# A hybrid attention, SSD and expert layer: final norm in pieces between the ninth unit's dots, last unit in groups of two and one, residual by TensorE, first loads in smaller steps

## The chip, the core and the metric

The kernel runs on one core of one Trainium2 chip. The metric is the device time of one execution in microseconds (us); the time of a kernel is the median of its runs. All data are 32-bit floats.

## The reference, cut to what matters

256 tokens of width 1024 go through one layer:

```python
mix = token_mix(x, positions, w_in, ...)      # top-k attention + SSD scan, then @ w_out
x = layer_norm(ALPHA * x + mix, ln1_g, ln1_b)
ffn = peer(x, peer_wq, k1, k2, u, v)          # 8 heads, 16 of 16384 experts each, per token
x = layer_norm(ALPHA * x + ffn, ln2_g, ln2_b)

# peer, per token: for each of 8 x 16 chosen experts e with gate g_e
ffn = sum_e gelu(dot(x, u[e])) * g_e * v[e]
```

Each token needs 128 rows of `u` and of `v`. The kernel keeps them side by side in HBM as one table `expert_uv`, a row of 2048 floats (8 KB) for each expert.

## The kernel before, in words

The tokens are two tiles of 128 (one token per partition). The projections, the attention and the SSD scan of tile 0 come first, and those of tile 1 are woven into the first expert units.

**Units and slots.** The expert part is 16 units (`UNITS`): unit u is head u % 8 of tile u // 8, with 16 slots. A slot is one gather (L459): an indirect DMA that POOL issues and that puts one 8 KB row into each of 128 partitions, into one of 16 places of `arena`. POOL waits before it until the place is free (`slot_used`, L457). DVE takes the dot of the row's first half with the token (L1548, `dot_slots`), ACT the gelu (L994) and the product with the gate (L999), each for a group of slots (`slot_groups`, L337: four groups of four, in the last unit 4, 4, 2, 2, 1, 1, 1, 1). ACT then scales the row's second half in place (L1009), and PE adds it into two PSUM banks of the tile by eight transposes against the identity (L659, `sum_slots`), which frees the place. In the program of DVE each unit begins with the routing of the next one (`route_sides`, `route_pairs`), some 10 us of short instructions, and then takes its dots.

**Units 9 to 14** run in a hardware loop on each engine (`LOOP_FIRST`, `LOOP_TURNS`), the others are written out.

**End of a tile.** The banks hold the sum transposed. ACT copies them out (`copy_sum`, L1016), PE transposes them back into banks 6 and 7 (`sum_back`, L669), DVE adds the scaled residual (`add_sum`, L1539) and takes statistics (`half_stats`, L1377), centres with the gain (`centre`, L1386), waits for ACT's root (`root_of_variance`, L947) and spreads (`spread`, L1394); SP stores. For tile 0 PE does this after all slots of unit 8 (L810 to L813) and DVE after the dots of unit 8 (L1607 to L1610). The gain and offset of this norm are loaded by SP, spread over 128 partitions by the DMA (L404, L405).

**The last unit** has no transposes. ACT makes a diagonal matrix of each slot's weights (L1006), and PE adds diagonal x row straight into banks 6 and 7 (`sum_last_slots`, L679), after `sum_back(1)` has opened them. Each of the 32 products runs as two passes, as do all products of 32-bit data here but the transposes, so the profile counts 64.

**The front.** SP loads the columns of x in four parts and the q weights in two halves (L371, L373) while ACT loads the index weights in four parts and nine small tensors; PE projects the index columns of tile 0, then of tile 1 (L692), waiting for a part at every second k (L487), and then q (L695). SP's further weight loads wait for all small tensors (L374 to L376).

## Time and profile before

| | |
|---|---|
| three runs, median (lowest to highest) | 805.42 us (805.28 to 806.05) |
| profiled execution, its own time | 807.17 us |
| its span | 805.4 us |
| busy: PE, DVE, ACT, POOL | 549.3, 548.6, 450.2, 283.9 us |
| moved by DMA | 301.08 MB, 374 GB/s over the span |
| mean granted TensorE clock | 0.843 of full speed |

Times in the profile are us from the span's start. PE's busy time are its matmul passes, PEld its weight loads. The DMA share is the mean busy share of 16 DMA engines. An idle time stands with what ended it; idle time of an engine that sets nothing costs nothing.

### The profile page before, as it was taken

What the parts mean: (1) busy time and instruction counts of PE and PEld (TensorE: products, weight loads), DVE (VectorE), ACT (ScalarE), POOL (GpSimd) and SP (SyncE); (2) the same over time, 40 slices, a digit from 0 to 9 for tenths busy, and PEclk for the clock granted to TensorE, in tenths of its full rate; (3) what the DMA queues carried; (4) which work ended last, traced back from release to release, by engine and by line L of the source; (5) the groups of instructions that cost most, each with busy time, mean ns of one, the idle gap of its engine ahead of it and who ended that gap; (6) DMA issues with size and microseconds to landing.
All of it is one profiled execution on the core that took longest, in us unless ns stands there. A gap on an engine that the chain in (4) does not pass through costs nothing.

```text
span 805.4 us, 10125 instructions
## 1 busy us (share of the span) xinstructions
PE 549.3 (68%) x3340; PEld 455.4 (57%) x3340; DVE 548.6 (68%) x1395; ACT 450.2 (56%) x805; POOL 283.9 (35%) x267
## 2 busy tenths in 40 slices
PE   7999999998957878565545454609554645454695
PEld 4486497776857778454445454608454644454642
DVE  3488487898654767676757576399767767676554
ACT  1125138778744666666565566529665656566532
POOL 0000004536613345444434444307644444444400
PEclk9999999999978989867878787758777668777689
DMA  7992017999999999999999999999999999999992
GB/s 258 390 392 90 0 54 239 422 421 421 422 418 421 420 421 420 421 421 422 419 422 420 422 421 422 421 422 360 421 421 422 423 422 421 422 423 422 422 422 111
DMA packets 51433, 301.08 MB, mean 374 GB/s; under 512 B 5696, under 2 KB 8000, under 8 KB 17600
## 3 DMA queue, kind: packets, MB, share of 16 engines
q0 software_dynamic: 36864, 268.45, 80.6%
q1 hardware_dynamic: 12144, 30.67, 10.2%
q10 hardware_dynamic: 2384, 1.44, 0.6%
q8 instruction: 22, 0.36, 0.2%
q14 instruction: 19, 0.16, 0.0%
HBM read 299.49 MB, written 1.05 MB: 373 GB/s over the span
## 4 chain that ended last, share of the span: by engine, by line
DMA 45%; DVE 20%; PE 19%; issue 8%; ACT 5%; POOL 3%; DVEq 0%; SPq 0%; another core or an unknown queue 0%; POOLq 0%; ACTq 0%
DMA arena<-in_expert_uv,expert 43%; PE bank L488 5%; DVE arena L1548 4%; PE bank L679 4%; PE bank L659 3%; POOL arena L459 3%; ACT arena L1009 2%; PE bank L500 2%; PE bank L603 2%; DMA ln_gb<-in_w_in 2%; ACT weight L999 1%; PE bank L622 1%; DVE score L1527 1%; DVE picked L1528 1%; DVE big L1258 1%
## 5 line engine op out<-in xcount | busy, mean ns | idle before, releaser
L659 PE MATMUL bank<-ident,arena 128*128 128x128 f32 x1920 | 299.2, 325 | 237.1 <-ACT arena L1009 235.7
L459 POOL DMA_INDIRECT arena<-in_expert_uv,expert x256 | 282.2, 1102 | 479.2 <-PE bank L659 261.9
L1548 DVE SCALAR_TENSOR_TENSOR arena<-x_sb,arena 128x1024 f32<-128x1024 f32 x256 | 307.0, 1224 | 172.6 <-DMA arena<-in_expert_uv,expert 165.1
L659 PEld LDWEIGHTS bank<-ident,arena 128*128 128x128 f32 x1920 | 275.1, 171 | 263.1 <-ACT arena L1009 258.6
L1009 ACT ACTIVATE arena<-arena,weight 128x1024 f32<-128x1024 f32 x240 | 257.5, 1141 | 2.2
L994 ACT ACTIVATE gelu<-dots 128x4 f32<-128x4 f32 (+2 forms) x76 | 15.6, 205 | 223.6 <-DVE arena L1548 214.4
L999 ACT ACTIVATE weight<-gelu,gate 128x1 f32<-128x1 f32 x256 | 56.1, 286 | 3.5
L488 PE MATMUL bank<-arena,x_t 128*128 128x512 f32 (+1 forms) x128 | 53.8, 576 | 4.8 <-DMA x_t<-in_x_columns 4.8
L488 PEld LDWEIGHTS bank<-arena,x_t 128*128 128x128 f32 x128 | 25.3, 203 | 27.0 <-issue 25.3
L622 PE MATMUL bank<-x_t,arena 128*128 128x128 f32 x256 | 29.9, 275 | 0.0
L679 PE MATMUL bank<-arena,mid 128*128 128x512 f32 x64 | 29.4, 622 | 0.0
L622 PEld LDWEIGHTS bank<-x_t,arena 128*128 128x128 f32 x256 | 29.2, 192 | 0.0
L500 PE MATMUL bank<-x_t,arena 128*128 128x128 f32 x256 | 29.0, 275 | 0.0
L500 PEld LDWEIGHTS bank<-x_t,arena 128*128 128x128 f32 x256 | 28.7, 192 | 0.1
L603 PE MATMUL bank<-arena,big 128*128 128x512 f32 x64 | 28.5, 592 | 0.0
L994 ACT ACT_TABLE_LOAD x19 | 24.4, 1283 | 0.6
L679 PEld LDWEIGHTS bank<-arena,mid 128*128 128x128 f32 x64 | 12.8, 202 | 15.9 <-issue 15.2
L1548 DVE DVE_READ_ACCUMULATOR arena<-x_sb,arena 128x1 f32 x256 | 21.2, 83 | 0.0
L357 ACT ACT_TABLE_LOAD x15 | 19.2, 1283 | 0.7
L603 PEld LDWEIGHTS bank<-arena,big 128*128 128x128 f32 x64 | 11.8, 190 | 12.9 <-issue 12.9
L622 PE MATMUL bank<-x_t,mix 128*128 128x128 f32 x128 | 15.1, 276 | 0.0
L622 PE MATMUL bank<-x_t,big 128*128 128x128 f32 x128 | 14.9, 275 | 0.0
(227 smaller groups left out, 488.9 us busy)
## 6 DMA issues: line engine op xcount, KB each, us to landing
arena<-in_w_in SPq DMA_DIRECT2D x5, 2048.0 KB, 17.5
arena<-in_w_out SPq DMA_DIRECT2D x2, 2048.0 KB, 19.3
arena<-in_expert_uv,expert POOLq DMA_INDIRECT x256, 28.1
arena<-in_peer_wq SPq DMA_DIRECT2D x4, 1024.0 KB, 9.4
mix<-in_peer_wq SPq DMA_DIRECT2D x2, 1024.0 KB, 5.2
big<-in_peer_wq SPq DMA_DIRECT2D x2, 1024.0 KB, 4.9
arena<-in_w_idx ACTq DMA_DIRECT2D x4, 304.0 KB, 5.7
x_t<-in_x_columns SPq DMA_DIRECT2D x4, 256.0 KB, 5.2
```

The lines of the kernel that those rows point to most:

```text
L357: nc.scalar.activation(gate_e[:, :], best[:, :], ACT.Exp, bias=neg_best[:, :], accum_out=gate_sum[:, :]).then_inc(gate_exp_ready, 1)
L459: pool.indirect_dma_start(out=arena[:, slot * SLOT:(slot + 1) * SLOT], out_offset=None, in_=expert_uv, in_offset=bass.IndirectOffsetOnAxis ...
L488: last = mm(bank(job)[:, 0:width], lhsT=x_t[:, k, t * P:(t + 1) * P], rhs=weight_rows(name, k, width), start=k == 0, stop=k == KT - 1)
L500: last = mm(bank(job)[:, c * P:(c + 1) * P], lhsT=weight_rows(f"xbc{n}", k)[:, c * P:(c + 1) * P], rhs=x_t[:, k, t * P:(t + 1) * P], start ...
L603: last = mm(bank(job)[:, :], lhsT=mix_t[t][:, k, :], rhs=weight_rows(f"out{half}", k), start=k == 0, stop=k == KT - 1)
L622: last = mm(bank(job)[:, n * P:(n + 1) * P], lhsT=head_weights(h)[:, k, n * P:(n + 1) * P], rhs=h_t[:, k, t * P:(t + 1) * P], start=k == 0 ...
L659: last = mm(banks[2 * tile + k // 4][:, (k % 4) * P:(k % 4 + 1) * P], lhsT=arena[:, at + k * P:at + (k + 1) * P], rhs=ident[:, :], is_tran ...
L679: last = mm(banks[SUM_BACK + half][:, :], lhsT=diag[:, j % 8, :], rhs=arena[:, at:at + 512], start=False, stop=j == SLOTS - 1, skip_group_ ...
L994: run(gelu[:, parity, part], dots[:, parity, part], ACT.Gelu).then_inc(gelu_ready, 1)
L999: done = run(weight[:, parity, j:j + 1], gelu[:, parity, j:j + 1], ACT.Copy, scale=gate[:, parity, j:j + 1])
L1009: run(arena[:, at:at + D_MODEL], arena[:, at:at + D_MODEL], ACT.Copy, scale=weight[:, parity, j:j + 1]).then_inc(scaled_ready, 1)
L1548: ins = stt(rows, x_rows[:, bass.ds(tile * D_MODEL, D_MODEL)], 1.0, rows, ALU.mult, ALU.mult, accum_out=dots[:, parity, j:j + 1])
```

## The change

It moves the final norm of tile 0 into unit 8's dots, changes the order and the group sizes of the last unit, gathers the last two slots' halves apart, lets PE add the residual as a product with ALPHA x identity, loads the final norm's vectors as four short rows that PE spreads over the partitions in unit 5, and loads the first operands in five parts, with q's weights laid out in HBM so that a partition's part is one piece of 8 KB.

```diff
@@ slot_groups, loads (SP; ACT's w_idx loads likewise)
                 elif u == UNITS - 1:
-                    sizes = (4, 4, 2, 2, 1, 1, 1, 1)
+                    sizes = (2,) * 4 + (1,) * 8
+        IDX_PARTS = [range(0, 1), range(1, 2), range(2, 4), range(4, 6), range(6, 8)]
-            for part in range(4):
-                ks = slice(2 * part, 2 * part + 2)
+            for part, some in enumerate(IDX_PARTS):
+                ks = slice(some[0], some[-1] + 1)
                 sp.dma_start(x_t[:, ks, :], ...).then_inc(idx_in[part], 16)
             for half in range(2):
-                sp.dma_start(q_halves[half], w_rows[:, 4 * half:4 * half + 4, Q0:Q0 + 512]).then_inc(w_in_sem["q"], 16)
+                sp.dma_start(q_halves[half], w_q[half].rearrange("p (k n) -> p k n", k=4)).then_inc(w_in_sem["q"], 16)
...
-            sp.wait_ge(ln1_done, 1)
-            sp.dma_start(ln_gb[:, 0, :], cast_rows(ln2_g)).then_inc(ln2_in, 16)
-            sp.dma_start(ln_gb[:, 1, :], cast_rows(ln2_b)).then_inc(ln2_in, 16)
+            sp.wait_ge(y_ready, TILES)
+            for n, source in enumerate((ln2_g, ln2_b)):
+                sp.dma_start(ln2_rows[2 * n:2 * n + 2, :], source.rearrange("(a b) -> a b", a=2)).then_inc(ln2_in, 16)
@@ POOL
-            gather_unit(UNITS - 1, 1)
+            gather_unit(UNITS - 1, 1, SLOTS - 2)
+            u, half_rows = UNITS - 1, expert_uv.rearrange("e (s d) -> (e s) d", s=2)
+            pool.wait_ge(last_rows_ready, 1)
+            for part in range(2):
+                for n in range(2):
+                    j = SLOTS - 2 + n
+                    at = slots_of(u)[j] * SLOT + part * D_MODEL
+                    if part == 0:
+                        pool.wait_ge(slot_used, (u - 1) * SLOTS + j + 1)
+                        pool.sem_inc(rows_asked, 1)
+                    pool.indirect_dma_start(
+                        out=arena[:, at:at + D_MODEL], out_offset=None, in_=half_rows,
+                        in_offset=bass.IndirectOffsetOnAxis(ap=last_rows[:, n, part:part + 1], axis=0),
+                    ).then_inc(last_values_in[n] if part else rows_in[slots_of(u)[j]], 16)
@@ PE
+            def add_residual(t):
+                pe.wait_ge(alpha_ready, 1)
+                for half in range(2):
+                    mm(banks[SUM_BACK + half][:, :], lhsT=alpha_ident[:, :], rhs=x_sb[:, t, half * 512:(half + 1) * 512],
+                       start=True, stop=False, skip_group_check=True)
...
+            def spread_ln2(part):
+                job = ("ln2", part)
+                pe.wait_ge(ln2_in, 2 * 16)
+                wait_bank(pe, job)
+                mm(bank(job)[:, :], lhsT=ident[0:4, part:part + 1].broadcast_to([4, P]), rhs=ln2_rows[0:4, :],
+                   start=True, stop=True).then_inc(full(job), 1)
...
-            for t in range(TILES):
-                project(("proj_idx", t), "idx", t, IDX_COLS + SSD_HEADS)
+            for part, some in enumerate(IDX_PARTS):
+                pe.wait_ge(idx_in[part], 32)
+                for t in range(TILES):
+                    project(("proj_idx", t), "idx", t, IDX_COLS + SSD_HEADS, ks=some)
...
-            sum_slots(PEER_HEADS, 1, first_unit=True)
+            sum_group(PEER_HEADS, 0)
             for n in range(4, PSUM_BANKS):
                 pe.wait_ge(bank_free[n], bank_uses[n])
+            add_residual(0)
             sum_back(0)
+            for g in range(1, 4):
+                sum_group(PEER_HEADS, g)
...
             pe.wait_ge(sum_added, 2)
+            add_residual(1)
+            sum_last_slots(UNITS - 1, range(0, 4))
             sum_back(1)
-            sum_last_slots(UNITS - 1)
+            sum_last_slots(UNITS - 1, range(4, SLOTS))
@@ ACT (copy_sum(1) stands after group 1 of the last unit, the root of tile 0 after group 2 of unit 8)
+            act.wait_ge(decay_masked, TILES)
+            run(alpha_ident[:, :], ident[:, :], ACT.Copy, scale=ALPHA).then_inc(alpha_ready, 1)
+            def take_ln2(part):
+                job = ("ln2", part)
+                wait_job(act, job)
+                act.wait_ge(ln1_done, 1)
+                run(ln_rows[:, part * 512:(part + 1) * 512], bank(job)[:, :], ACT.Copy).then_inc(free(job), 1)
...
@@ DVE (add_sum is gone; centre reads the banks for the final norm)
+            def sum_stats(t, half):
+                dve.wait_ge(half_back[half], 1 + 2 * t)
+                link(nc.vector.bn_stats(stats[:, 6 * half:6 * half + 6], banks[SUM_BACK + half][:, :]))
...
+                crossing = isinstance(u, int) and u == PEER_HEADS
                 for g in range(len(slot_groups(u))):
                     dot_slots(u, tile, parity, g)
                     if g == 0 and not last:
                         finish_gate(u + 1, 1 - parity)
+                    if crossing and g == 1:
+                        sum_stats(0, 0)
+                    if crossing and g == 2:
+                        sum_stats(0, 1)
+                        dve.wait_ge(ln2_ready, 4)
+                        centre(0, summed=True)
+                if crossing:
+                    spread(0, TILES, result_ready)
...
+            for part in range(2):
+                ins = ts(last_rows[:, :, part], expert[:, 1, SLOTS - 2:], 2.0, float(part), ALU.mult, ALU.add)
+            ins.then_inc(last_rows_ready, 1)
             dot_unit(UNITS - 1, TILES - 1, 1)
             for half in range(2):
-                half_stats(TILES - 1, half, add_sum)
-            normalise(TILES - 1, 2 * TILES - 1, result_ready)
+                sum_stats(TILES - 1, half)
+            normalise(TILES - 1, 2 * TILES - 1, result_ready, summed=True)
```

PE's `spread_ln2(g)` stands before group g of unit 5, ACT's `take_ln2(g)` behind it. In `sum_last_slots` slots 14 and 15 wait besides for `last_values_in`.

## Rows read from the trace of the kernel before

**Rows 1.** The page: the chain that ended last, by engine; the gathers' issue.
```profile
DMA 45%; DVE 20%; PE 19%; issue 8%; ACT 5%; POOL 3%; DVEq 0%; SPq 0%; another core or an unknown queue 0%; POOLq 0%; ACTq 0%
...
arena<-in_expert_uv,expert POOLq DMA_INDIRECT x256, 28.1
```

**Rows 2.** Windows: length; busy PE, PEld, DVE, ACT, POOL; clock; DMA share, GB/s.
```profile
300.00:400.00 100.00, 62.98 (x427) 59.16 (x425) 68.60 (x179) 64.53 (x109) 47.66 (x44) 0.81 1.01 421
545.00:550.00 5.00, 5.00 (x28) 5.00 (x27) 5.00 (x11) 4.93 (x10) 3.23 (x2) 0.54 0.75 264
550.00:555.00 5.00, 4.46 (x42) 4.22 (x41) 5.00 (x9) 4.93 (x9) 4.39 (x3) 1.00 1.00 370
555.00:560.00 5.00, 3.92 (x32) 3.13 (x31) 4.24 (x24) 4.93 (x10) 3.78 (x4) 1.00 0.97 383
```

**Rows 3.** Timeline at the crossing: start, length (us), engine, line, operation [idle before <-releaser].
```profile
490.82 1.06 ACT L1016 ACTIVATE mix<-bank 128x512 f32<-128x512 f32 x2
...
519.83 1.04 PE L669 MATMUL bank<-ident,mix 128*128 128x128 f32 x8
...
520.54 0.69 DVE L1539 SCALAR_TENSOR_TENSOR x_sb<-x_sb,bank 128x512 f32<-128x512 f32 x1 [9.03 <-issue]
...
536.58 1.23 DVE L1548 SCALAR_TENSOR_TENSOR arena<-x_sb,arena 128x1024 f32<-128x1024 f32 x1
...
546.47 1.66 POOL L459 DMA_INDIRECT arena<-in_expert_uv,expert  x1 [24.35 <-PE bank L659]
```

**Rows 4.** DMA issues: loads of ln_gb; the window behind the second pair.
```profile
ln_gb<-in_ln_g SPq DMA_DIRECT2D x2, 512.0 KB, 11.6
...
230.00:235.00 5.00, 0.00 (x0) 0.00 (x0) 1.23 (x2) 0.00 (x0) 0.00 (x0) 0.71 1.02 424
```

**Rows 5.** Timeline of the last unit and the tail.
```profile
755.53 6.46 PE L659 MATMUL bank<-ident,arena 128*128 128x128 f32 x32 [3.63 <-ACT arena L1009]
...
764.32 1.28 ACT L1006 ACTIVATE mid<-ident,weight 128x128 f32<-128x128 f32 x4
...
766.23 1.94 PE L669 MATMUL bank<-ident,mix 128*128 128x128 f32 x8 [4.25 <-ACT mix L1016]
...
767.96 29.36 PE L679 MATMUL bank<-arena,mid 128*128 128x512 f32 x64
...
791.65 1.23 DVE L1548 SCALAR_TENSOR_TENSOR arena<-x_sb,arena 128x1024 f32<-128x1024 f32 x1 [1.21 <-DMA arena<-in_expert_uv,expert]
...
793.48 0.40 ACT L1006 ACTIVATE mid<-ident,weight 128x128 f32<-128x128 f32 x1
...
796.50 0.69 DVE L1539 SCALAR_TENSOR_TENSOR x_sb<-x_sb,bank 128x512 f32<-128x512 f32 x1 [3.62 <-PE bank L679]
...
799.62 0.21 DVE L1383 BATCH_NORM_AGGREGATE moments<-stats 128x2 f32<-128x12 f32 x1
```

**Rows 6.** Windows of one us around PE's last transposes and its first weighted passes.
```profile
760.00:761.00 1.00, 1.00 (x7) 1.00 (x6) 0.61 (x2) 0.00 (x0) 0.99 (x1) 0.50 1.00 418
761.00:762.00 1.00, 0.98 (x8) 0.74 (x6) 0.14 (x1) 0.00 (x0) 0.70 (x2) 0.91 1.01 418
768.00:769.00 1.00, 1.00 (x3) 0.48 (x3) 0.06 (x2) 0.00 (x0) 0.00 (x0) 0.50 1.04 434
```

**Rows 7.** Timeline of the front.
```profile
4.81 11.12 PE L488 MATMUL bank<-arena,x_t 128*128 128x304 f32 x32 [4.81 <-DMA x_t<-in_x_columns]
...
12.67 0.17 DVE L1160 CAST pos_f<-pos_i 128x2 f32<-128x2 int32 x1 [12.67 <-DMA arena<-in_inv_freq]
...
16.32 3.70 PE L488 MATMUL bank<-x_sb,x_t 128*128 128x512 f32 x8 [0.39 <-DMA ln_gb<-in_w_in]
...
16.87 15.11 SPq L364 DMA_DIRECT2D arena<-in_w_in  x5
...
30.36 0.69 DVE L1185 TENSOR_TENSOR arena<-bank,sin_cos 128x512 f32<-128x512 f32 x1 [3.50 <-PE bank L488]
```

**Rows 8.** Window in which the q weights land.
```profile
12.00:14.00 2.00, 2.00 (x10) 1.47 (x9) 1.22 (x8) 0.00 (x0) 0.00 (x0) 1.00 0.95 315
```

More of the change, by code:

```diff
@@ L71, in psum_jobs @@
         jobs += [("peer_q", 0, h), ("key_scores", 0, h), ("peer_q", 1, h), ("key_scores", 1, h)]
-    return jobs
+    return jobs + [("ln2", part) for part in range(4)]
 def bank_plan():
@@ L218, in build_layer @@
         expert = ctx.enter_context(nc.sbuf_tensor("expert", [P, 2, 16], i32))
+        last_rows = ctx.enter_context(nc.sbuf_tensor("last_rows", [P, 2, 2], i32))
+        alpha_ident = upper
         gate_e, gate_sum = sb("gate_e", 16), sb("gate_sum", 1)
@@ L230, in build_layer @@
         x_in = sem("x_in")
-        idx_in = [sem(f"x_t_and_idx_in{part}") for part in range(4)]
+        IDX_PARTS = [range(0, 1), range(1, 2), range(2, 4), range(4, 6), range(6, 8)]
+        idx_in = [sem(f"x_t_and_idx_in{part}") for part in range(len(IDX_PARTS))]
         w_names = ["q", "k", "xbc0", "xbc1", "v", "z", "out1", "out0"] + [f"wq{h}" for h in range(PEER_HEADS)]
@@ L258, in build_layer @@
         SUM_BACK = 6
+        last_rows_ready, alpha_ready = sem("last_rows_ready"), sem("alpha_ready")
+        last_values_in = [sem(f"last_values_in{n}") for n in range(2)]
         result_ready, out_stored = sem("result_ready"), sem("out_stored")
@@ L439, in gather_unit @@
                     pool.wait_ge(experts_ready, u + 1)
-                for j, slot in enumerate(slots_of(u)):
+                for j, slot in enumerate(slots_of(u)[:n]):
                     if isinstance(u, int) and u == 0 and j == 8:
@@ L669, in sum_back, with sum_last_slots @@
                         last = mm(banks[SUM_BACK + half][:, n * P:(n + 1) * P], lhsT=sum_t[:, 4 * half + n, :], rhs=ident[:, :],
-                                  is_transpose=True, start=n == 0, stop=t == 0, skip_group_check=True)
+                                  is_transpose=True, start=False, stop=t == 0, skip_group_check=True)
                     last.then_inc(half_back[half], 1)
-            def sum_last_slots(u):
-                for j in range(SLOTS):
+            def add_residual(t):
[3 more added lines that the diff above has]
+                       start=True, stop=False, skip_group_check=True)
+            def sum_last_slots(u, some):
+                for j in some:
                     pe.wait_ge(diag_ready, j + 1)
+                    if j >= SLOTS - 2:
+                        pe.wait_ge(last_values_in[j - SLOTS + 2], 16)
                     for half in range(2):
@@ L803, in _ @@
                         queries(*now)
+                    if u == LN2_UNIT:
+                        spread_ln2(g)
                     sum_group(u, g)
@@ L817, in _ @@
             pe.wait_ge(sum_added, 2)
+            add_residual(1)
+            sum_last_slots(UNITS - 1, range(0, 4))
             sum_back(1)
-            sum_last_slots(UNITS - 1)
+            sum_last_slots(UNITS - 1, range(4, SLOTS))
         @block.scalar
         def _(act):
-            for part in range(4):
-                ks = slice(2 * part, 2 * part + 2)
+            for part, some in enumerate(IDX_PARTS):
+                ks = slice(some[0], some[-1] + 1)
                 act.dma_start(chunk(places["idx"], IDX_COLS + SSD_HEADS)[:, ks, :],
@@ L1024, in weigh_unit @@
                     weigh_slots(u, parity, g)
-                    if last and g == 0:
+                    if last and g == 1:
                         copy_sum(TILES - 1)
@@ L1028, in weigh_unit @@
                         copy_sum(0)
+                    if isinstance(u, int) and u == PEER_HEADS and g == 2:
+                        root_of_variance(TILES)
             take_index_dots(0)
@@ L1431, in _ @@
             for half in range(2):
-                half_stats(0, half, add_mixed)
+                half_stats(0, half)
             normalise(0, 0, h_ready)
@@ L1534, in finish_gate @@
                 ts(gate[:, parity, :], gate_e[:, :], gate_sum[:, :], None, ALU.mult).then_inc(gate_ready, 1)
-            def add_sum(t, half, part):
-                dve.wait_ge(half_back[half], 1 + 2 * t)
-                link(stt(x_sb[:, t, part], x_sb[:, t, part], ALPHA, banks[SUM_BACK + half][:, :], ALU.mult, ALU.add))
-                dve.sem_inc(sum_added, 1)
             def dot_slots(u, tile, parity, g):
@@ L1592, in _ @@
             for half in range(2):
-                half_stats(1, half, add_mixed)
+                half_stats(1, half)
             centre(1)
@@ L1605, in _ @@
                 dot_unit(u, u // PEER_HEADS, u % 2)
-                per_unit = count[0] - before + 1
-            dve.wait_ge(ln2_in, 32)
-            for half in range(2):
-                half_stats(0, half, add_sum)
-            normalise(0, TILES, result_ready)
+                if u < PEER_HEADS:
+                    per_unit = count[0] - before + 1
             dve.wait_ge(scores_ready, len(score_order))
```

36 lines of the change are left out of this document (22 added, 14 removed).

## The prediction

> **What bounds the kernel now.** I read the page's chain first [rows 1]: its largest share is DMA, which is the gathers of expert rows, and a gather lands 28.1 us after its issue, so some eleven are queued at once. The windows show whether that queue runs dry [rows 2]: over 300 to 400 us the DMA share is 1.01 at 421 GB/s while PE is busy 63 and DVE 69 of 100 us. A gather moves 128 rows of 8 KB, 1.05 MB, so one lands every 1.05 / 0.421 = 2.49 us. From there to the end the time is bytes over 421 GB/s. An edit pays there only if it removes bytes or refills a dry queue. What lies ahead of the first gather (compute) and behind the last one (the tail) counts in full.
>
> The same view shows one dry place: in 545 to 560 us the rate is 264, 370 and 383 GB/s [rows 2]. The timeline says why [rows 3]. DVE has no dot left after unit 8 and waits 9.03 us for the sum that PE hands back only after all of unit 8; it normalises, routes unit 10, and takes its next dot at 536.58. Slots are freed only after dots, so POOL's next issue waits 24.35 us.
>
> In the tail [rows 5] the last row lands at 791.65, its diagonal is ready at 793.88, but PE's string of 64 weighted passes runs from 767.96 without a gap to 797.32: there PE is the bound. It starts late because it stands behind the copy of the sum (ACT), which stands behind the first group of four.
>
> In front [rows 7], PE starts at 4.81 when the first index parts land, ends them at 15.93, and waits for the q weights until 16.32.
>
> A measurement of this kernel can tell about 0.2% (1.6 us) from no change.
>
> **The change, part by part.** Signs: minus is time saved.
>
> Middle norm. Missing bytes in the three windows: (421-264)x5 + (421-370)x5 + (421-383)x5 = 1230 KB, at 421 GB/s 2.9 us. After the change DVE's work is two BN_STATS, one aggregate, one add, two centring and two spreading passes, some 5 us, laid between unit 8's dots. A dot takes 1.23 us of each 2.49 us [rows 5], so 1.25 us per slot is free. The new wait is DVE's for the first half of the sum, behind group 1. ACT's copy starts at 490.82 [rows 3], PE then has its last scaled slot, four residual passes (0.43 us each, 0.85 at half clock; working below) and the turned-back transposes (1.04 us): ready at about 495.5 to 498, and DVE is there at about 491.7. Behind the wait stand dots 8 to 15, which are due from 492.9 on; they start 3 to 6 us late, and the eight of them regain up to 10 us. Nothing is late by group 3, except that unit 9's routing starts about 1.7 us later (the spreading). The cover is the queue: in the old kernel DVE was without dots for 25 us and this cost 2.9 us, so delays below some 22 us cost nothing. The root's two table loads on ACT are hidden in the same way. Ends: 0 (the stall comes back elsewhere) and -2.9; I take **-2.9**.
>
> Final norm's vectors. Before, two loads of 512 KB [rows 4] go through the full queue: in the five us behind their issue the rate is 424 GB/s at a share of 1.02 [rows 4]. Now four short rows come in and PE spreads them in unit 5. 2 x 524 KB / 421 GB/s = **-2.5 us**. Added: four 512-column products on PE and four copies on ACT of about 0.6 us, covered by PE's and ACT's idle time and the queue; without cover about 6 us. Ends: -2.5 and 0.
>
> Last unit. The time of one weighted pass: at the full clock 0.43 us, since 64 take 29.36 us with the first few at half clock (the window at 768 shows 0.50 [rows 6]); 64 x 0.43 = 27.5, so the slow start cost 1.9 us. A slot is 4 passes, 1.72 us. After the change PE goes on at 761.99, when its transposes of unit 14 end [rows 5], with four residual passes, slots 0 to 3 (diagonals at about 760 and 764), the turned-back sum, and the rest. Continuous work would end at 762.0 + 68 x 0.43 + 1.04 = 792.3, so it catches up with the data. Two things could then end last. Slot 13: a diagonal is ready 2.28 us behind its landing (791.65 to about 793.9), two gathers earlier than slot 15's: 788.95. From there slots 13, 14 and 15 take 3 x 1.72 and end at 794.1. The value halves: the last lands at 791.65 as before (same bytes), the one before it 1.25 us earlier, 790.4 + 3.44 = 793.8. The later counts; its first half bank is complete 0.86 us earlier, at 793.25. Before, DVE began at 796.50. **-3.2 us**. POOL's two further issues (about 0.94 us each, at 762 to 767) lie 25 us ahead of their landings. Its new wait for the row numbers is answered before unit 15's dots, so nothing queues behind it. Ends: -3.5, and -1.3 if PE pays the 1.9 us of slow clock again.
>
> The clock. In the old trace PE's transposes start at 755.53; the granted clock is 0.50 at 760 and 0.91 at 761 while only transposes run [rows 6]. The new residual passes follow at once, at the full level of 2.4 GHz. The Trainium skill (TensorE: Matmul & The Clock Gate, Part 4: PE-mode transpose) says that transposes do not count as busy for the gate. By that rule the residual would start at 1.2 GHz and the tail gain be 1.3 us instead of 3.2; the rows at 760 and 761 speak against it.
>
> The split gathers. Their price is not in this trace: no gather has 4 KB rows. Lower end nothing (the same bytes), upper end that a half takes as long as a whole one, 2 x 2.49 = +5.0 us. I take 0, since the nearest row, the window of q's loads with their 2 KB rows [rows 8], still shows three quarters of the rate with many small loads beside them, and the norm vectors' loads, with rows of 4 KB, left the rate at 424 GB/s [rows 4]. The Trainium skill (DMA: Bandwidth & Descriptors, Rules for kernel authors) asks for at least 1 MiB per DMA, and (section Anatomy of one DMA) gives some 2.0 us of fixed cost for each on the GpSimd path; paid in series by four halves that would be an estimated +8 us. Gathers here land 2.49 us apart although each needs 28.1 us, so such a cost overlaps.
>
> Residual by PE. Before: scale-add, statistics, scale-add, statistics from 796.50, aggregate at 799.62: 3.12 us. Now statistics read the bank: 0.69 us on half 0 while PE ends half 1 (0.86 us later), then 0.69 and small gaps: 1.6 us. **-1.5 us**; the centring reads PSUM, as the old scale-add did at 0.69 us. Ends -1.6 and -1.2.
>
> First loads. The first parts are half as large, so PE may start about 0.7 us earlier (a first pair of parts is 560 KB, at 315 to 421 GB/s 1.3 to 1.8 us, and half of it falls away) and end the index products near 15.2 by its 11.1 us of passes. Contiguous q weights: 2.1 MB at 315 GB/s [rows 8] is 6.7 us, at 421 it would be 5.0, so q lands near 14.6 to 15.5. PE starts q at about 15.4. SP and ACT each issue one load more, some 0.5 us, ahead of everything behind them; the queues are busy then, and SP's next issue waits for small loads until 16.87 anyway. Ends: +0.5 (a late last part) and -1.3; I take **-0.9**. It passes to the first gather, since the way there is compute.
>
> Sum: 2.9 + 2.5 + 3.2 + 1.5 + 0.9 = 11.0 us. The profiled execution took 807.17 us (span 805.4): 796.2. The three runs' median is 1.75 us lower, so 794.4.
>
> **Rivals.**
> 1. PE still bounds the tail (a half-clock spell or waits between small groups). For: 68 passes against 2.49 us per slot leave little; the clock stood at 0.50 at 768, after 4.25 us without work [rows 5, 6]. Against: PE has a backlog from 762 on. 2 to 3 us of the tail gain go: 796.4 to 797.4.
> 2. The stall at the crossing stays, because DVE waits for PE inside unit 8. For: a new chain ACT, PE, DVE. Against: 22 us of cover. 797.3.
> 3. Half gathers cost as much as whole ones: +5.0, 799.4. For: rows cost something each. Against: above.
> 4. Slower than before: the large q packets hold back ACT's small loads (positions, frequencies, keys), which share the engines. Place: DVE's first instruction at 12.67, SP's wait that ends at 16.87 [rows 7]. DVE has 3.50 us of idleness at 30.36, so the small loads must land over 3.5 us later to cost anything, and over 3.5 + 10.1 + 1.6 = 15.2 us later (behind about 28 us) to make the kernel slower. At most the 2.1 MB of q stand ahead of them, 5.0 us at 421 GB/s. Time with 17 us of delay: 794.4 + 0.9 + 17 - 3.5 = 808.8.
> 5. The change does not remove the bytes' cost (the load ran in spare bandwidth). Against: share 1.01. 796.9.
>
> **How the numbers follow.** Forecast 0.70, its own range 792.5 to 796; rival 1 0.13, rival 2 0.06, rival 3 0.05, rival 5 0.02, rival 4 0.02, and 0.02 that small losses together leave no difference. The range reaches from 792.0 (front at its best, tail at -3.5, and half a us for the sum) to 798.5, over rivals 1, 2 and 5, short of rival 3. Faster by over 0.2%: 0.96; within: 0.02; slower: 0.02.
>
> **What would show it.** Right: no window under 410 GB/s between 300 us and the last gathers; POOL's longest wait near 8 us in place of 24.35; 1 MB fewer bytes moved; from the last landing to the first store's issue some 4.7 us less than before; PE's q products start near 15.4; at the end PE shows short waits on DMA or on diagonals. Wrong: a gap of POOL over 15 us near unit 9, a granted clock of 0.5 within 20 us of the end, gathers in the last 5 us at under 350 GB/s, or an index part landing after 13.5 us.

## The result and the profile after

| | before | after |
|---|---|---|
| four runs each on one chip, median (lowest to highest) | 805.73 us (805.28 to 806.45) | 799.60 us (799.24 to 800.43) |
| profiled execution, its own time (span) | 807.17 us (805.4) | 799.47 us (797.7) |
| moved by DMA | 301.08 MB | 300.04 MB |
| mean granted TensorE clock | 0.843 | 0.853 |

The ratio on record is 0.9917 (95% interval 0.9904 to 0.9930); the two medians shown stand as 0.9924, 6.1 us apart. The forecast was 794.4 us in a range of 792.0 to 798.5: the sign was right, the time 1.1 us above the range. Between the two profiled executions the gain is 7.7 us; the profile of before lies 1.4 us above the median of its runs, that of after 0.1 us under its own.

**Where the 7.7 us lie.** The rows of DVE's dots are good milestones, since each dot waits for its row. From the timelines of both kernels I collected the starts of some:

```
start of DVE's dot (us)      before   after    shift
first dot of all             129.92   129.66   -0.26
unit 1, slot 15              216.61   216.20   -0.41
unit 3, slot 15              308.69   305.79   -2.90
unit 7, slot 15              470.57   467.07   -3.50
unit 8, slot 15              510.28   506.82   -3.46
unit 10, slot 15             592.91   589.41   -3.50
unit 15, slot 12             784.23   780.78   -3.45
DVE begins last statistics   796.50   790.14   -6.36
DVE aggregates them          799.62   791.81   -7.81
```

So the front gives 0.4 us, the stretch with the norm's vectors (from unit 1's slot 15 to unit 3's) 2.5, units 4 to 7 0.6, the last unit 2.9 and the statistics 1.5. The crossing (units 8 to 10), which I had counted on, gives nothing.

**The page after**: the chain by engine; POOL's gathers with their busy time and what ended POOL's idle time; the gathers' issues (KB and time to landing are not given where they vary).

```profile
DMA 54%; PE 17%; DVE 16%; issue 6%; ACT 4%; POOL 2%; SPq 0%; DVEq 0%; POOLq 0%; ACTq 0%
...
L467 POOL DMA_INDIRECT arena<-in_expert_uv,expert x254 | 275.6, 1085 | 479.8 <-PE bank L678 265.4
...
arena<-in_expert_uv,expert POOLq DMA_INDIRECT x254
...
arena<-in_expert_uv,last_rows POOLq DMA_INDIRECT x4, 26.2
```

DMA holds 54% of the chain, where it held 45% [rows 1]; PE 17% and DVE 16%, where they held 19% and 20%. The gathers still bound the middle. Nine points of the span are some 70 us, though, and the kernel is 7.7 us shorter: most of the shift is the chain going through the gathers where it went through PE and DVE before, not work that is gone.

**The crossing after**, windows as in [rows 2]:

```profile
540.00:545.00 5.00, 2.64 (x13) 2.64 (x14) 2.47 (x5) 4.90 (x9) 0.80 (x1) 0.50 1.02 423
545.00:550.00 5.00, 2.80 (x21) 2.56 (x19) 2.53 (x5) 0.46 (x2) 3.48 (x4) 0.91 1.03 428
550.00:555.00 5.00, 2.70 (x15) 2.70 (x16) 4.24 (x24) 4.93 (x9) 1.08 (x2) 0.78 1.02 423
555.00:560.00 5.00, 2.68 (x19) 2.44 (x17) 4.61 (x13) 3.33 (x5) 3.42 (x4) 0.88 1.01 413
```

and the timeline there, as in [rows 3]:

```profile
492.00 0.70 DVE L1442 BATCH_NORM_STATS2 stats<-bank 128x6 f32<-128x512 f32 x1 [3.80 <-PE bank L688]
...
498.06 0.70 DVE L1442 BATCH_NORM_STATS2 stats<-bank 128x6 f32<-128x512 f32 x1
...
499.11 1.40 DVE L1450 SCALAR_TENSOR_TENSOR x_sb<-bank,moments,ln_gb 128x512 f32<-128x512 f32 x2
...
519.00 1.23 DVE L1608 SCALAR_TENSOR_TENSOR arena<-x_sb,arena 128x1024 f32<-128x1024 f32 x1
...
528.88 1.99 POOL L467 DMA_INDIRECT arena<-in_expert_uv,expert  x1 [9.94 <-PE bank L678]
```

The change does here what it says. DVE takes the first half's statistics at 492.00 between dots, centres from the banks at 499.11, and takes unit 9's first dot at 519.00, where it was 536.58. POOL's wait before the first gather of unit 10, its 161st in both kernels, is 9.94 us where it was 24.35 (near 8 was forecast). The windows at 545 to 560 us, which stood at 264, 370 and 383 GB/s, stand at 428, 423 and 413. And the stretch from unit 8's slot 15 to unit 10's is 82.59 us where it was 82.63: the 1.2 MB that had seemed missing had cost no time.

**The norm's vectors**, the window where [rows 4] had their two loads of 512 KB:

```profile
230.00:235.00 5.00, 0.00 (x0) 0.00 (x0) 1.71 (x3) 0.00 (x0) 0.00 (x0) 0.69 1.01 419
```

The rate is the same, and 1.04 MB less goes through it in all.

**The tail after**, as in [rows 5], and two windows of one us as in [rows 6]:

```profile
752.09 6.37 PE L678 MATMUL bank<-ident,arena 128*128 128x128 f32 x32 [3.71 <-ACT arena L1054]
...
758.30 1.88 PE L696 MATMUL bank<-x_sb,upper 128*128 128x512 f32 x4
...
760.01 7.03 PE L707 MATMUL bank<-arena,mid 128*128 128x512 f32 x16
...
766.88 1.04 PE L688 MATMUL bank<-ident,mix 128*128 128x128 f32 x8
...
767.75 12.33 PE L707 MATMUL bank<-arena,mid 128*128 128x512 f32 x28
...
785.54 5.42 PE L707 MATMUL bank<-arena,mid 128*128 128x512 f32 x12 [0.50 <-ACT mid L1051]
...
785.70 1.23 DVE L1608 SCALAR_TENSOR_TENSOR arena<-x_sb,arena 128x1024 f32<-128x1024 f32 x1
...
790.14 0.70 DVE L1442 BATCH_NORM_STATS2 stats<-bank 128x6 f32<-128x512 f32 x1 [3.20 <-PE bank L707]
...
791.81 0.21 DVE L1446 BATCH_NORM_AGGREGATE moments<-stats 128x2 f32<-128x12 f32 x1
```

```profile
756.00:757.00 1.00, 1.00 (x6) 1.00 (x6) 1.00 (x1) 0.55 (x2) 0.42 (x1) 0.50 0.98 410
757.00:758.00 1.00, 1.00 (x9) 1.00 (x8) 0.18 (x2) 0.00 (x0) 0.98 (x1) 0.71 0.98 410
```

PE's weighted products begin at 760.01 (before: 767.96) and the first 16 passes take 7.03 us, at the full clock. Its backlog ends with slot 10; it waits 0.50 us for slot 13's diagonal at 785.54, and the last twelve passes take 5.42 us. DVE's first half is ready at 790.14, its second 0.93 us later, and it aggregates 1.67 us after it began, where it needed 3.12. The last dot starts at 785.70, 5.95 us earlier than before. The clock stood at half level (1.2 GHz) through the first five us of transposes and rose to the full level (2.4 GHz) within 757 to 758 us, while PE had done nothing but transposes since 752.09; the residual's products, which start at 758.30, had it from the first (the windows from 758 on show 1.00). The rule of the Trainium skill (TensorE: Matmul & The Clock Gate, Part 4: PE-mode transpose) that transposes do not bring up the clock is contradicted by the row at 757, as by [rows 6]: this case's 32-bit transposes had the clock at 0.71 there, and at 1.00 in the next window.

**The front after**, PE's rows, as in [rows 7]:

```profile
3.80 3.69 PE L507 MATMUL bank<-arena,x_t 128*128 128x304 f32 x8 [3.80 <-DMA x_t<-in_x_columns]
8.34 4.36 PE L507 MATMUL bank<-arena,x_t 128*128 128x304 f32 x16 [0.85 <-DMA arena<-in_w_idx]
13.73 2.31 PE L507 MATMUL bank<-arena,x_t 128*128 128x304 f32 x8 [1.04 <-DMA arena<-in_w_idx]
16.16 2.41 PE L507 MATMUL bank<-x_sb,x_t 128*128 128x512 f32 x5
```

PE starts 1.01 us earlier, and has lost 0.85 and 1.04 us of it again in waits for index weights: it ends them at 16.04, where it was 15.93, and starts q at 16.16 instead of 16.32.

### The profile page after: what moved, and what is told of

Its sections match the earlier page's. It is cut to its first block, busy times and chain, and to the rows that moved or that the text cites. A ratio compares the mean times of both kernels' runs of the same rounds, so it can differ in the third digit from the quotient of the medians.

```text
span 797.7 us, 10181 instructions
## 1 busy us (share of the span) xinstructions
PE 553.0 (69%) x3356; PEld 455.3 (57%) x3356; DVE 546.5 (69%) x1393; ACT 454.5 (57%) x815; POOL 281.1 (35%) x269
## 2 busy tenths in 40 slices
DMA packets 50705, 300.04 MB, mean 376 GB/s; under 512 B 5732, under 2 KB 8036, under 8 KB 16872
## 4 chain that ended last, share of the span: by engine, by line
DMA 54%; PE 17%; DVE 16%; issue 6%; ACT 4%; POOL 2%; SPq 0%; DVEq 0%; POOLq 0%; ACTq 0%
DMA arena<-in_expert_uv,expert 53%; PE bank L507 5%; PE bank L678 4%; DVE arena L1608 3%; POOL arena L467 2%; PE bank L519 2%; PE bank L622 2%; ACT arena L1054 2%; DMA ln_gb<-in_w_q 2%; ACT weight L1044 1%; PE bank L641 1%; DVE big L1317 1%; PE bank L707 1%; PE bank L499 1%; DVE score L1591 1%
## 5 line engine op out<-in xcount | busy, mean ns | idle before, releaser
L467 POOL DMA_INDIRECT arena<-in_expert_uv,expert x254 | 275.6, 1085 | 479.8 <-PE bank L678 265.4
L707 PEld LDWEIGHTS bank<-arena,mid 128*128 128x128 f32 x64 | 11.7, 190 | 17.6 <-issue 11.9
L622 PEld LDWEIGHTS bank<-arena,big 128*128 128x128 f32 x64 | 11.8, 190 | 12.9 <-issue 12.9
L641 PE MATMUL bank<-x_t,mix 128*128 128x128 f32 x128 | 15.1, 276 | 0.0
L641 PE MATMUL bank<-x_t,big 128*128 128x128 f32 x128 | 14.9, 275 | 0.0
```

Source lines behind the costliest of these rows:

```text
L467: pool.indirect_dma_start(out=arena[:, slot * SLOT:(slot + 1) * SLOT], out_offset=None, in_=expert_uv, in_offset=bass.IndirectOffsetOnAxis ...
L622: last = mm(bank(job)[:, :], lhsT=mix_t[t][:, k, :], rhs=weight_rows(f"out{half}", k), start=k == 0, stop=k == KT - 1)
L641: last = mm(bank(job)[:, n * P:(n + 1) * P], lhsT=head_weights(h)[:, k, n * P:(n + 1) * P], rhs=h_t[:, k, t * P:(t + 1) * P], start=k == 0 ...
L707: last = mm(banks[SUM_BACK + half][:, :], lhsT=diag[:, j % 8, :], rhs=arena[:, at:at + 512], start=False, stop=j == SLOTS - 1, skip_group_ ...
```

## The experiments

Each edit is made on the kernel after; the kernel before ran beside each group of four on the same chip (medians 806.33, 806.73 and 806.41 us). What an execution costs in front turned out to scatter, so stretches between dots of the profiled executions are compared beside the medians.

### The kernel after, run twice more, and the norm of the crossing put back

`r1_after_again` and `r9_after_third` have no edit.

> The changed kernel once more, as the yardstick of this group. Both theories: 799.6 us, within 0.8 us; a span of about 797.7 us.

> The changed kernel as the yardstick of this group: ratio to the kernel before 0.992 to 0.993. Where its profile shows index products that wait 2 us or more before their last part, the granted clock falls to half behind them, q starts near 18.5 us and the span is some 2.4 us longer than with waits of 1 us.

Measured: 800.69 us (799.95 to 802.05), ratio 0.9930 [0.9913, 0.9946], and 799.79 us (799.55 to 800.11), ratio 0.9913 [0.9896, 0.9931]. With the first result, three medians of this kernel lie within 1.1 us; r1's is 0.3 us outside what was expected of it. That is the noise under which all differences between groups stand.

`r2_norm_behind_unit8` puts PE's, ACT's and DVE's steps of tile 0's norm behind all of unit 8, as before the change:

```diff
-            sum_group(PEER_HEADS, 0)
+            sum_slots(PEER_HEADS, 1, first_unit=True)
             ...
             add_residual(0)
             sum_back(0)
-            for g in range(1, 4):
-                sum_group(PEER_HEADS, g)
@@ DVE
-                    if crossing and g == 1:
-                        sum_stats(0, 0)
-                    if crossing and g == 2:
-                        sum_stats(0, 1)
-                        dve.wait_ge(ln2_ready, 4)
-                        centre(0, summed=True)
                 if crossing:
+                    for again in range(REPEAT):
+                        sum_stats(0, 0)
+                    sum_stats(0, 1)
+                    dve.wait_ge(ln2_ready, 4)
+                    centre(0, summed=True)
                     spread(0, TILES, result_ready)
```

ACT's root goes back behind the unit too. `REPEAT` is 1 there, and 9 in `r3_norm_behind_unit8_and_pause`: eight more statistics of the same bank, some 5.8 us in which DVE takes no dot.

> The changed kernel with tile 0's final norm put back behind unit 8's dots (PE hands the sum back after all slots of unit 8, DVE waits for it there). Theory A, free stall: the dip of the mean rate at the crossing never held up a landing, because the DMA engine that finishes each gather last still had work; the time is that of the changed kernel, within 0.6 us, although the windows near unit 9 show a dip below 400 GB/s again. Theory B, the forecast's: a dry queue costs what its missing bytes cost; the time is 2.9 us longer than the changed kernel's, about 802.5 us.

> As the run before, and DVE takes the statistics of half 0 nine times instead of once, 8 x 0.72 = 5.8 us more without a dot. Theory A: POOL's gap of about 24 us was within some 2 us of the point where the last DMA engine would have run dry, so 5.8 us more cost about 4 us: 803.5 us. Theory B: each us of pause costs a us from the start: 799.6 + 2.9 + 5.8 = 808.3 us. Theory C, the cover is much wider than the queue: 799.6 us again.

Measured: r2 800.12 us (798.72 to 801.15), ratio 0.9922 [0.9903, 0.9941]; r3 804.23 us (802.48 to 805.39), ratio 0.9973 [0.9963, 0.9984]. The windows and POOL's longest wait of r2, then of r3:

```profile
540.00:545.00 5.00, 3.71 (x22) 3.71 (x23) 5.00 (x11) 4.94 (x9) 0.93 (x1) 0.59 0.82 342
545.00:550.00 5.00, 4.77 (x40) 3.98 (x39) 5.00 (x9) 4.94 (x9) 4.09 (x4) 1.00 0.77 269
...
544.07 1.67 POOL L467 DMA_INDIRECT arena<-in_expert_uv,expert  x1 [24.45 <-PE bank L678]
```

```profile
540.00:545.00 5.00, 0.00 (x0) 0.00 (x0) 4.96 (x11) 2.21 (x7) 0.00 (x0) 0.50 0.80 334
545.00:550.00 5.00, 4.95 (x23) 4.95 (x24) 5.00 (x11) 4.93 (x9) 1.87 (x2) 0.50 0.08 34
550.00:555.00 5.00, 5.00 (x43) 4.89 (x41) 5.00 (x9) 4.93 (x10) 4.39 (x3) 0.90 0.96 341
...
547.83 1.66 POOL L467 DMA_INDIRECT arena<-in_expert_uv,expert  x1 [29.82 <-PE bank L678]
```

In r2 the dip is back, 342 and 269 GB/s, 1.16 MB short of 421, and the kernel isn't slower than r1 (800.69). From unit 8's slot 15 to unit 10's it needs 82.69 us; before, after and all runs but r3 need 82.59 to 82.70, with the dip or without. In r3 one window more is all but empty (34 GB/s), and the same stretch is 86.23 us: 5.8 us of pause cost 3.6 us there, and 3.5 us in the median against r1, 4.1 against r2. So the old stall stood about 2.2 us short of costing anything, if all of the pause beyond that edge counted; one length of pause was run. The first theory holds. The DMA share of 0.77 says that some of the 16 engines had run dry, but the landings, which DVE waits for, did not come later.

What stands behind it shows in the landing records of the traces, though no run was made for it. Each gather is reported in 16 parts (its semaphore goes up by 16), which I take to be one from each engine, and it has landed with the last. The lead of the first and of the fifteenth part over the last, in gathers with all parts recorded that landed at 530 to 545 us (before) and at 560 to 600 us (behind):

| | first part, before and behind the crossing | fifteenth part, before and behind |
|---|---|---|
| kernel before | 6.5 us, 2.7 us | 2.5 us, 0.7 us |
| r2 | 6.9, 3.0 | 3.1, 1.3 |
| r3 | 5.7, 1.9 | 1.4, 0.3 |
| kernel after (no dip) | 6.0, 7.0 | 1.8, 2.1 |

Where there is a dip, the parts that ran ahead lose their lead, and the last one comes when it did without the dip. So the missing bytes were lead that no dot used. In r3 the window at 34 GB/s shows all engines all but idle, and only from there on does the last part come later too. Why one part stays behind, and which engine it is, is not shown. The Trainium skill (DMA: Bandwidth & Descriptors, Latency and other measured facts) notes that two of the sixteen are usually slower, and gives its reason as a guess; no run here can tell whether that is the cause.

### The norm's vectors

`r4_norm_vectors_spread_by_dma` loads them as before, two times 512 KB, and takes PE's products and ACT's copies out:

```diff
-                sp.dma_start(ln2_rows[2 * n:2 * n + 2, :], source.rearrange("(a b) -> a b", a=2)).then_inc(ln2_in, 16)
+                sp.dma_start(ln_gb[:, n, :], cast_rows(source)).then_inc(ln2_in, 16)
```

> The changed kernel with the final norm's vectors loaded as before, 512 KB each over all partitions, without PE's and ACT's part in unit 5. If bytes count in full: 2.5 us longer than the changed kernel, about 802.1 us, and the first dots behind the load late by as much. If the load runs in spare bandwidth: 799.6 us.

Measured: 802.38 us (800.94 to 803.42), ratio 0.9957 [0.9943, 0.9971]: 1.7 us over r1, 2.3 over r2. From unit 1's slot 15 to unit 3's it takes 92.62 us, and before 92.08; after and the eleven other runs take 89.25 to 90.37. The difference is 2.3 to 3.4 us for r4, and 2 x 524 KB at 421 GB/s are 2.5. So these bytes count in full, as was expected; that they do so because the slowest engine gets its share of them too is argued and not shown. The four products and copies cost nothing that shows.

### The front

`r5_q_in_2kb_rows` takes q from `w_in` again (each partition's part in rows of 2 KB), `r6_q_behind_index_parts` keeps the 8 KB pieces but lets SP wait for the fourth index part before it issues q, `r10_front_as_before` restores the whole front:

```diff
@@ r5, and r10
-                sp.dma_start(q_halves[half], w_q[half].rearrange("p (k n) -> p k n", k=4)).then_inc(w_in_sem["q"], 16)
+                sp.dma_start(q_halves[half], w_rows[:, 4 * half:4 * half + 4, Q0:Q0 + 512]).then_inc(w_in_sem["q"], 16)
@@ r6, ahead of the two loads
+            sp.wait_ge(idx_in[3], 32)
@@ r10
-        IDX_PARTS = [range(0, 1), range(1, 2), range(2, 4), range(4, 6), range(6, 8)]
+        IDX_PARTS = [range(n, n + 2) for n in range(0, KT, 2)]
-            for part, some in enumerate(IDX_PARTS):
-                pe.wait_ge(idx_in[part], 32)
-                for t in range(TILES):
+            for t in range(TILES):
+                for part, some in enumerate(IDX_PARTS):
+                    pe.wait_ge(idx_in[part], 32)
```

> The changed kernel with q's weights read from w_in again, in pieces of 2 KB instead of 8 KB. Theory A, large pieces hold back the index parts that ACT's queue loads: PE's index products run without the waits of 0.85 and 1.04 us and end near 15 us instead of 16.0, but q lands near 16.2 as before the change, so PE starts q at 16.2 to 16.4 and the time stays within 0.4 us; the small loads land near 13 instead of 16.5 us. Theory B, the pieces have no part in it: the index products end at 16.0 again and q starts later still, at about 17: 0.9 us longer.

> The changed kernel, but SP waits for the fourth of the five index parts before it issues the q loads (8 KB pieces kept). Theory A: the index parts are not held back, the index products end near 14.9, q lands near 15.5 and PE starts it there, 0.6 us earlier than in the changed kernel; the time is 0.6 us shorter. Theory B: no gain in the index products, and q lands later than 16.2: 0.5 us or more longer.

> The changed kernel with the whole front as before: four index parts, tile by tile, q in 2 KB pieces. Theory A, the new front brings about nothing and loses 2.4 us in those executions in which PE's clock falls: q starts near 16.3 at full clock every time, the time is that of the changed kernel's better executions, 0 to 1.5 us shorter in the median, with less scatter. Theory B, the new front is a gain as forecast: 0.9 us longer.

Measured: r5 802.36 us (801.11 to 803.60), ratio 0.9941 [0.9924, 0.9958]; r6 802.54 us (801.16 to 805.12), 0.9954 [0.9938, 0.9970]; r10 800.30 us (799.73 to 801.68), 0.9918 [0.9900, 0.9936], beside r9's 799.79. PE's rows of r1 (the kernel after), with two windows behind them, then of r5, then of r6:

```profile
14.95 3.91 PE L507 MATMUL bank<-arena,x_t 128*128 128x304 f32 x8 [2.06 <-DMA arena<-in_w_idx]
18.66 3.73 PE L507 MATMUL bank<-x_sb,x_t 128*128 128x512 f32 x8
```

```profile
15.00:16.00 1.00, 1.00 (x3) 0.77 (x4) 0.00 (x0) 0.00 (x0) 0.00 (x0) 0.75 0.52 127
16.00:17.00 1.00, 1.00 (x3) 0.67 (x2) 0.51 (x4) 0.00 (x0) 0.00 (x0) 0.50 0.02 3
```

```profile
8.48 6.41 PE L507 MATMUL bank<-arena,x_t 128*128 128x304 f32 x24 [0.82 <-DMA arena<-in_w_idx]
17.18 5.40 PE L507 MATMUL bank<-x_sb,x_t 128*128 128x512 f32 x8 [2.29 <-DMA ln_gb<-in_w_in]
```

```profile
3.83 11.29 PE L508 MATMUL bank<-arena,x_t 128*128 128x304 f32 x32 [3.83 <-DMA x_t<-in_x_columns]
17.54 3.70 PE L508 MATMUL bank<-x_sb,x_t 128*128 128x512 f32 x8 [2.41 <-DMA ln_gb<-in_w_q]
```

Three things are to be seen. First, q's large pieces do hold back ACT's loads: with them the last index part ends a wait at 13.73 (after), 14.95 (r1) and 12.59 (r9); in r5 and r6, where q has 2 KB rows or waits, the index products end near 14.9 and 15.1 and the last part is never waited for (by the landing records it is in place at 11.8 and 10.9). Second, that buys nothing, because then q is late: it lands at 17.1 and 17.5, where it lands at 14.4 to 16.1 in the nine runs with the front of the kernel after, and PE stands 2.29 and 2.41 us before it. What the index weights gain, q loses. So r5's first theory had the index products right and q wrong, and of r6's two the second came, a later q. No kernel after ran in their group, so their medians are not compared with its medians. Third, such a wait of some two us can be followed by half clock (1.2 GHz): in r1 the window 16 to 17 us shows 0.50 and the last eight index passes take 3.91 us where they took 2.31; r5 shows it too (5.40 us for eight q passes, some 3.7 elsewhere), and so does the front of r7 after 2.03 us of waiting; r6 does not, after a wait as long. No other profile has such a wait over 1.42 us in front, and none of them shows half clock at 14 to 20 us. First dots stand at 132.18 (r1), 132.38 (r5) and 132.08 (r7) with the half clock, and at 129.66 (after), 129.19 (r9), 131.02 (r6) and 130.29 (r10) without. These 2 to 3 us are one source of the scatter between executions of one kernel.

r2, r3, r4, r7, r8 and r11 leave the front as it is in the kernel after, so there are nine profiles of it. Seven kept the full clock, and their first dots stand at 128.63 to 129.66, 129.3 in the mean; the old front has 129.92 (before) and 130.29 (r10). So the new front is worth some 0.8 us where the clock holds, near the 0.9 of the forecast, and it loses some 2.8 in the two where it fell (r1, r7). r10's median, 0.5 us over r9's, lies between its two theories and doesn't tell them apart.

`r12_q_by_halves` follows from this. PE lacks work between the index products and q's last row, so let it begin q with the rows that are there: 2 KB rows as in r5, a semaphore of its own for each half, and both tiles' k 0 to 3 before k 4 to 7:

```diff
-                sp.dma_start(q_halves[half], w_q[half].rearrange("p (k n) -> p k n", k=4)).then_inc(w_in_sem["q"], 16)
+                sp.dma_start(q_halves[half], w_rows[:, 4 * half:4 * half + 4, Q0:Q0 + 512]).then_inc(w_in_sem[("q", "q_late")[half]], 16)
-            pe.wait_ge(w_in_sem["q"], 32)
-            for t in range(TILES):
-                project(("proj_q", t), "q", t)
+            for half, name in enumerate(("q", "q_late")):
+                pe.wait_ge(w_in_sem[name], 16)
+                for t in range(TILES):
+                    project(("proj_q", t), "q", t, ks=range(4 * half, 4 * half + 4))
```

> The changed kernel with its five index parts, q in 2 KB pieces, and PE taking the first half of q's rows for both tiles as soon as that half has landed. Theory A, what the front lacks is work between the index products and q's last row: PE runs from about 3.8 us without a wait over 1 us, the clock doesn't fall, q starts near 15 us, and the time is 1 to 1.5 us shorter than with the front as before. Theory B, the front's length is not on the path to the first gather: the same time as with the front as before.

Measured: 798.02 us (797.66 to 798.39), ratio 0.9893 [0.9875, 0.9911]; every run is under every run of r9 (799.55 to 800.11) on the same chip, 1.8 us in the median. It is faster than both kernels.

```profile
8.07 6.41 PE L507 MATMUL bank<-arena,x_t 128*128 128x304 f32 x24 [0.41 <-DMA arena<-in_w_idx]
14.40 7.13 PE L507 MATMUL bank<-x_sb,x_t 128*128 128x512 f32 x16
```

PE passes from the index products to q at 14.40 without a wait, and the first dot stands at 127.90, 1.3 us before r9's. The first theory came; against r10 the gain is 2.3 us, where 1 to 1.5 was expected. Compared with r9, q's rows are new as well as the halves; r5 has these rows without the halves, on another chip, and its first dot came at 132.38 with half clock. The halves with 8 KB pieces were not run.

### The last unit

`r7_old_groups` restores the group sizes with the copy behind the first group, `r8_whole_last_gathers` gathers slots 14 and 15 whole, `r11_sum_back_first` turns the order of PE's steps:

```diff
@@ r7 (and ACT's copy of the sum behind group 0)
-                    sizes = (2,) * 4 + (1,) * 8
+                    sizes = (4, 4, 2, 2, 1, 1, 1, 1)
@@ r8 (the four half gathers and their semaphores go)
-            gather_unit(UNITS - 1, 1, SLOTS - 2)
+            gather_unit(UNITS - 1, 1)
@@ r11
-            sum_last_slots(UNITS - 1, range(0, 4))
             sum_back(1)
-            sum_last_slots(UNITS - 1, range(4, SLOTS))
+            sum_last_slots(UNITS - 1, range(0, SLOTS))
```

> The changed kernel with the last unit's groups as before (4, 4, 2, 2, 1, 1, 1, 1) and ACT's copy of the sum behind the first. Theory A, the tail hangs on slot 13's diagonal: PE starts its weighted products about 1 us later, works that off before slot 13 and ends at the same time: within 0.4 us of the changed kernel. Theory B, PE's backlog reaches to the end: PE has no idle time left before slot 13, and the end comes 1 us or more later.

> The changed kernel with slots 14 and 15 gathered whole. Theory A: the last row lands when the last value half landed; dot, diagonal (2.28 us) and products (1.7 us) follow it, so PE ends 1.0 to 1.5 us later and the time is as much longer. Theory B, half gathers cost extra time in the queue: the last row lands earlier than the last half did, and the time is the same or shorter.

> The changed kernel with the sum turned back ahead of the first four weighted slots. PE waits for ACT's copy, some 2 us after the residual, and starts its weighted products 3 us later; it has 1.5 us of waits left ahead of slot 13 to make up. Theory A: 1.5 to 2.5 us longer than the changed kernel. Theory B, the tail hangs on slot 13's diagonal alone: within 0.4 us.

Measured: r7 802.02 us (800.64 to 804.32), r8 801.67 us (801.11 to 802.15), both 0.9936 [0.9920, 0.9953]; r11 799.85 us (799.42 to 801.68), 0.9920 [0.9898, 0.9942]. No kernel after ran in the group of r7 and r8, so their tails are judged by the stretch from slot 12's dot to DVE's last statistics, which the front doesn't touch: before 12.27 us, after 9.36, r1 9.35, r7 10.48, r8 10.82, r11 9.33. PE's rows and windows of r7, its rows of r8, then of r11:

```profile
765.08 8.83 PE L707 MATMUL bank<-arena,mid 128*128 128x512 f32 x16 [2.15 <-ACT mid L1051]
...
766.00:768.00 2.00, 2.00 (x4) 0.86 (x3) 0.87 (x1) 0.86 (x2) 0.70 (x1) 0.59 1.02 426
768.00:770.00 2.00, 2.00 (x4) 0.79 (x3) 0.75 (x3) 0.00 (x0) 0.00 (x0) 0.56 0.98 406
...
774.95 20.87 PE L707 MATMUL bank<-arena,mid 128*128 128x512 f32 x48 [0.17 <-ACT mid L1051]
```

```profile
788.94 1.98 PE L692 MATMUL bank<-arena,mid 128*128 128x512 f32 x4 [0.47 <-ACT mid L1036]
791.40 1.98 PE L692 MATMUL bank<-arena,mid 128*128 128x512 f32 x4 [0.47 <-ACT mid L1036]
```

```profile
762.17 1.15 PE L688 MATMUL bank<-ident,mix 128*128 128x128 f32 x8 [1.79 <-ACT mix L1060]
763.15 22.48 PE L707 MATMUL bank<-arena,mid 128*128 128x512 f32 x52
786.02 5.42 PE L707 MATMUL bank<-arena,mid 128*128 128x512 f32 x12 [0.39 <-ACT mid L1050]
```

In r7 PE waits 2.15 us for the first diagonals, its first weighted passes run at 0.59 and 0.56 of the clock (16 take 8.83 us where they took 7.03), and it never catches up (48 passes without a gap from 774.95 on): 1.1 us, the second theory. In r8 PE waits half a us at every slot and the last slot is bound by its own diagonal, at 791.40: 1.5 us, the first theory. So the split gathers pay, and they cost nothing that shows: from unit 10's slot 15 to unit 15's slot 12 all fourteen profiles need 191.3 to 191.5 us. In r11 the late copy makes PE wait 1.79 us before the weighted passes, and it still comes to slot 13 in time (0.39 us of wait at 786.02): the order is worth nothing by itself, given the small groups, as its second theory had it.

## Why the prediction was right and wrong

By its own steps, in time of the profiled executions, where it gave 11.0 us and 7.7 came:

1. **Middle norm, -2.9: it was 0.** This is the step that failed. It took the bytes that three windows lacked, divided them by the full rate and put the result down as time. A mean rate tells how many engines are busy, not whether a landing comes late; r2 has the dip without the cost (82.69 us across the crossing, 82.59 in the kernel after). Its own later sentence, that "delays below some 22 us cost nothing", was nearer: the stall itself was a delay that the queue covered, except that I took the dip as proof that the cover had ended. r3 puts the end of the cover about 2 us beyond the old stall. Rival 2 gave 797.3 for this term's loss, by another mechanism (a stall that stays); that stall did go.
2. **Norm's vectors, -2.5: it was -2.5** to unit 3 (1.7 in r1 and r9, which are the same kernel), and r4 gives 1.7 to 2.3 in the median. Right, and for the reason given, bytes through a full queue; that the number agrees to a tenth is luck.
3. **Last unit, -3.2: it was -2.9.** Slot 13's diagonal was the bound, as worked out, half a us of PE's idleness ahead of it; three slots took 5.42 us where 5.16 were counted. Rival 1 (PE bounds) did not come; r7 shows it when the small groups go. Rival 3 (half gathers cost as whole ones) was wrong; r8 shows that they gain 1.5. The clock stood at its full level when the residual came, as the rows at 760 and 761 had said.
4. **Residual by PE, -1.5: it was -1.5** (3.12 to 1.67 us).
5. **First loads, -0.9: it was -0.3 to the first dot and -0.4 to unit 1's slot 15.** The start 1.0 us earlier was right (0.7 was forecast). The end near 15.2 was wrong: "or an index part landing after 13.5 us" was on the list of what would make it wrong, and one ended a wait at 13.73. Rival 4's mechanism was there, but on the index weights instead of the small loads, and for one or two us where it needed over 15.2 to make the kernel slower. The small term of one pair of profiles is in part chance: over seven profiles at full clock the new front gives 0.8 us. What the term lacked is the clock, which r1 and r7 show to cost 2 to 3 us after the new wait, where nothing of it stood among the ends.
6. Units 4 to 7 gave 0.6 us that no step had (161.88 to 161.28 us from unit 3's slot 15 to unit 7's). It can't be told from scatter: the kernel after needs 161.15 in r1 and 162.04 in r9.

Of the 3.3 us between 11.0 and 7.7, the first step has 2.9, the third 0.3, the fifth 0.5, some 0.1 lies behind the aggregate, and the scatter of units 4 to 7 gave 0.6 back. A second gap is as large as a term: 7.7 us between the two profiles are 6.1 between the medians. Taking 1.75 us off supposed that what made before's profiled execution long lay where the change touches nothing. What made it long is open, and so is whether the terms read from it were too large for a usual execution. Executions of one kernel in the runs here differ by 0.6 (r9) to 4.0 us (r6), and the first dot of after's three profiles by 3.0; a sum against one execution should carry that as width, on both sides. The range had half a us for it. Its lower end doesn't follow from its own terms either: the front at its best, the tail at -3.5 and half a us give 794.4 - 0.4 - 0.3 - 0.5 = 793.2, not 792.0. Its upper end reached over one rival at a time and not over several terms that fail together, which is what came.

Of the signs that were named, the bytes came as said (1.04 MB fewer), and from 300 to 780 us no window of 5 us is under 410 GB/s. POOL's longest wait there is 9.94 us. One sign of being wrong came, gathers in the last 5 us at under 350 GB/s: 783 to 788 us stand at 103 GB/s (before, 786 to 791: 285). It cost no landing: rows went on landing every 2.49 us and halves every 1.24. The parts of a gather that lead have all landed and the last ones follow, so this sign has the fault of the first step, a mean rate read as time. From the last landing to the first store's issue it takes 6.48 us (788.17 to 794.65), and before 10.72 (791.63 to 802.35): 4.2 us less, where 4.7 was said. PE's q products started at 16.16 instead of near 15.4.

## What to carry to other kernels

A dip in the DMA rate is not yet a cost: look at the consumer's waits or starts on both sides of it, and only a shift there is time. Where a transfer is reported in parts, see how far they lie apart before and behind the dip. Where the queue stays full, bytes removed count at the full rate. In a tail where one unit's steps end each other's waits, work out the finish of the last few pieces one by one, and where PE waits for a last operand, split its work by what has landed before you reorder the transfers.

## What the runs showed of the hardware that was not expected

- A stall of the gathers that left 1.16 MB out of 10 us (r2: 342 and 269 GB/s) moved no dot behind it (82.69 us to unit 10's slot 15, 82.59 without the stall); 5.8 us more moved them by 3.6 (r3). The first of a gather's 16 parts led the last by 6.9 us before the stall and by 3.0 behind it (r2), and by 6.0 and 7.0 where there was none (after).
- With 8 KB pieces of q beside 1.2 KB pieces of the index weights, the last part of the latter landed at 12.6 to 14.9 us and q at 14.4 to 16.1 (nine profiles); with 2 KB rows of q and the same five parts it was 11.7 to 11.8 and 17.1 to 17.3 (r5, r12).
- After a wait of 2.06 us (r1), 2.03 and 2.15 us (r7, in front and in the tail) and 2.29 us (r5) PE ran at about half clock (windows at 0.50 to 0.59) for some 3 to 4 us; after 2.41 us in r6 it did not. What decides is open.
